# Who makes the low parts of the split weight blocks under the HGRN levels: VectorE or GpSimd

## The reference, cut to what matters

```python
def hgrn2_chunk_scan(q, k, logf, v):      # S_t = diag(f_t) S_{t-1} + k_t v_t^T, o_t = S_t^T q_t
...
    b = jnp.cumsum(fb, axis=2)
    decay = jnp.exp(jnp.where(incl, b_t - b_s, -jnp.inf))
    scores = jnp.einsum('nhtk,nhsk,nhtsk->nhts', qb, kb, decay)
    intra = jnp.einsum('nhts,nhsv->nhtv', scores, vb)
...
def hybrid_mixer(xn, w_in, ...):
    proj = jnp.einsum('bld,dc->blc', xn, w_in)
    q, zf_fwd, zf_bwd, inp, og, hy, gates = jnp.split(proj, IN_SPLITS, axis=-1)
```

## Time and profile before

| | |
|---|---|
| Times of the runs | 2528.5, 2533.27, 2532.15 us (median 2532.15) |
| Span of the profiled execution | 2527.7 us, first to last instruction |
| Busy share of TensorE, VectorE, ScalarE, GpSimd | 94%, 66%, 53%, 30% |
| Low parts by VectorE, line 343 | 398, of them 12 under the HGRN levels |
| Low parts by GpSimd, line 349 | 276 |

### The profile page before, as it was taken

One profiled execution on the slowest core, in us unless ns is written; L12 is line 12 of the kernel. 1 busy time (PEld: TensorE's weight loads), 2 busy tenths in 40 slices (PEclk: granted clock), 3 DMA queues, 4 the chain that ended last, 5 costly groups with the idle time before them and its releaser, 6 DMA issues.

```text
span 2527.7 us, 39068 instructions
## 1 busy us (share of the span) xinstructions
PE 2372.7 (94%) x15354; PEld 2141.8 (85%) x15354; DVE 1658.8 (66%) x3195; ACT 1342.3 (53%) x2494; POOL 770.8 (30%) x404
## 2 busy tenths in 40 slices
PE   6878998999999999998888888999999999999998
PEld 5876888999999888887867876789999999888886
DVE  4564457967777566665657475666977788566665
ACT  3344444468888444444533454244458888444443
POOL 3000002877776000000700053101887777000000
PEclk8888899999999999999999998999999999999999
DMA  5322334555555566664332343245555555566663
GB/s 175 122 94 70 94 99 153 176 177 165 165 163 170 179 192 193 190 191 140 117 122 87 125 135 109 67 150 159 184 176 162 165 162 163 184 192 192 191 193 123
DMA packets 108286, 383.36 MB, mean 152 GB/s; under 512 B 12975, under 2 KB 15840, under 8 KB 107528
## 3 DMA queue, kind: packets, MB, share of 16 engines
q1 hardware_dynamic: 108104, 380.86, 48.4%
HBM read 379.74 MB, written 1.06 MB: 151 GB/s over the span
## 4 chain that ended last, share of the span: by engine, by line
PE 81%; DVE 11%; ACT 4%; DMA 2%; issue 2%; POOL 0%; SPq 0%; DVEq 0%; ACTq 0%; POOLq 0%
PE psum L370 23%; PE psum L372 22%; PE psum L371 22%; PE psum L2042 2%; PE psum L402 2%; DVE weight_parts L343 2%; ACT weight_parts L338 1%; PE psum L616 1%; PE psum L2707 1%; PE psum L2487 1%; PE psum L1468 1%; PE psum L1029 1%; PE psum L1369 0%; PE psum L1199 0%; PE psum L1791 0%
## 5 line engine op out<-in xcount | busy, mean ns | idle before, releaser
L349 POOL TENSOR_TENSOR weight_parts<-weight_ring,weight_parts 128x1024 fp32r<-128x1024 f32 x276 | 670.5, 2440 | 505.7 <-ACT weight_parts L338 505.3
L370 PE MATMUL psum<-acts_high,weight_parts 128*128 128x256 f32 x2744 | 793.8, 289 | 22.4 <-DVE weight_parts L343 10.5
L372 PE MATMUL psum<-acts_high,weight_parts 128*128 128x256 f32 x2744 | 782.2, 285 | 0.0
L371 PE MATMUL psum<-acts_low,weight_parts 128*128 128x256 f32 x2744 | 781.8, 285 | 0.0
L338 ACT ACTIVATE weight_parts<-weight_ring 128x1024 fp32r<-128x1024 f32 x674 | 709.8, 1054 | 128.4 <-PE psum L372 60.7
L343 DVE TENSOR_TENSOR weight_parts<-weight_ring,weight_parts 128x1024 fp32r<-128x1024 f32 x398 | 487.6, 1226 | 306.6 <-ACT weight_parts L338 306.5
L370 PEld LDWEIGHTS psum<-acts_high,weight_parts 128*128 128x128 f32 x2744 | 531.6, 194 | 33.7 <-issue 12.5
L371 PEld LDWEIGHTS psum<-acts_low,weight_parts 128*128 128x128 f32 x2744 | 532.1, 194 | 1.3 <-issue 0.5
L372 PEld LDWEIGHTS psum<-acts_high,weight_parts 128*128 128x128 f32 x2744 | 532.0, 194 | 0.0
L370 PE MATMUL psum<-weight_parts,peer_coef 128*128 128x512 f32 x1024 | 404.0, 394 | 4.0 <-issue 3.9
L371 PE MATMUL psum<-weight_parts,peer_coef 128*128 128x512 f32 x1024 | 401.7, 392 | 0.0
(11 more groups left out here) (426 smaller groups left out, 3137.5 us busy)
## 6 DMA issues: line engine op xcount, KB each, us to landing
weight_ring<-in_peer_down SPq DMA_DIRECT2D x128, 512.0 KB, 3.6
weight_ring<-in_peer_up SPq DMA_DIRECT2D x128, 512.0 KB, 4.2
weight_ring<-in_peer_u SPq DMA_DIRECT2D x128, 512.0 KB, 3.6
weight_ring<-in_peer_v SPq DMA_DIRECT2D x128, 512.0 KB, 3.6
weight_ring<-in_w_in SPq DMA_DIRECT2D x88, 512.0 KB, 3.6
weight_ring<-in_w_out SPq DMA_DIRECT2D x16, 512.0 KB, 3.6
weight_ring<-in_peer_w_q SPq DMA_DIRECT2D x16, 512.0 KB, 4.1
weight_ring<-in_w_in_v SPq DMA_DIRECT2D x10, 512.0 KB, 3.5
```

The costliest lines, as they stand in the source:

```text
L349: q.e.tensor_tensor(self.low, self.ring, self.high.bitcast(F32), ALU.subtract).then_inc(*self.unit.ready.once())
L370: q.e.matmul(out, sh, mh, start=first, stop=False)
L371: q.e.matmul(out, sh, ml, start=False, stop=False)
L372: return q.e.matmul(out, sl, mh, start=False, stop=last)
```

## The change

`low_by` is set to "pool" before the units of `more()` are planned, and no longer only in `finish()`. So the 12 low parts under the levels go from VectorE's list to GpSimd's, at the same places between the rounds. Which blocks are whole, the loads, the roundings and the products stay as they were. `finish()` returns the mark of the last product, not that of the last product of a whole block.

```diff
+            c.low_by = "pool"
+
             def in_turns(units):
 
                 for n, _ in enumerate(units):
...
                 for _ in filler:
                     pass
                 c.whole = False
-                c.low_by = "pool"
                 c.flush(w[32], w[40])
-                return xn.whole_free
+                return c.last_product
```

## The result

| | before | after |
|---|---|---|
| median | 2531.63 us (6 runs, 2528.5 to 2534.11) | 2538.54 us (6 runs, 2536.17 to 2539.53) |
| span of the profiled execution | 2527.7 us | 2534.7 us |
| ratio, with its 95% interval | | 1.0033 [1.002, 1.0045] |

The forecast was +7.1 us, range 2530 to 2544; slower by over 0.2% had a chance of 0.58.

A forecast was written before the change was run, and what follows sets the result against it. The prediction took the chain of waits through VectorE's list to the second scores as the bound. Three pairs (1.1, 1.8, 1.65), the end (0.9) and TensorE's clock (1.65) gave +7.1 us, about 2539.2 us, range 2530 to 2544.

The forecast's parts named there:

- The bound: In the levels no engine is full; a chain of waits through load, rounding and VectorE's list to the second scores bounds.
- What is removed: 12 VectorE low parts of 1.14 us; second masked copy ends at T+4.9, not T+8.6 (T: end of a whole product).
- What is added: 12 GpSimd operations of 2.4 us, each costing VectorE 2.2 us of standing still where it meets parts or multiplications.
- The steps of pairs 2, 3 and 4 and the end: Second scores later by 1.1, 1.8 and 1.65 us in the three pairs; late low parts at the end add 0.9 us.
- TensorE's clock: Longer idle gap ahead of second scores makes the one quick pair slow (1.2 GHz): 1.40 plus 0.25, so +1.65 us.
- The total: +7.1 us on 2532.15, about 2539.2 us; +5.45 us without the clock's term.
- A: Rival: GpSimd's low parts cause no standing still that matters on VectorE; -4.4 us, 2527.7; chance 0.12.
- B: Rival: VectorE keeps its turn inside a run, GpSimd waits for the run's end; -1.4 us, 2530.8; chance 0.14.

The follow-up runs named there:

- Experiment 1: Kernel before with only the 4 low parts between the masked copies moved to GpSimd: ratio 0.9990 [0.998, 1.0001], stage 134.73 us for 138.88.
- experiment 5: Changed kernel, but each pair's third low part on GpSimd also waits for VectorE's last multiplication: ratio 1.0002 [0.999, 1.0013] to the kernel before.
- experiment 3: Kernel before with only the 3 low parts behind the multiplications (units 20, 26, 32) moved to GpSimd: ratio 1.0009 [0.9993, 1.0025].
- experiment 12: Repeat of experiment 3's kernel (only the 3 low parts behind the multiplications on GpSimd, against the kernel before): ratio 1.0002 [0.9989, 1.0014].
- experiment 2: Kernel before with only the 2 low parts behind the 8 parts (units 24, 30) moved to GpSimd: ratio 1.0008 [0.9993, 1.0023].
- experiments 6 to 8: Unread matmuls in TensorE's gaps, added to the changed kernel, the kernel before, and experiment 1's kernel: ratios to the kernel before 1.0038, 1.0014, 0.9986.
- experiments 9 to 11: Fewer unread matmuls, fitted to TensorE's gaps, in the changed kernel, the kernel before, and experiment 1's kernel: ratios to the kernel before 1.0034, 0.9996, 0.9985.

## Why the prediction was right

- **The bound.** The loop of load, rounding, copies, parts, exponentials, multiplications and scores sets the stage, and GpSimd's free time was no measure of the change's worth. Experiments 1 and 5 move the second scores by the amounts walked from it.
- **What is removed.** The second masked copy ended 3.7 us earlier in offsets from T, as said: 1346.49 against T = 1341.6 in the changed kernel. Experiment 1 keeps that gain and gives 1.0 to 1.6 us a pair.
- **What is added.** Standing still of 2.2 us: seven operations of the changed kernel took 3.28 to 3.42 us for 1.22, so 2.1 to 2.2. One place went otherwise, the eighth part of pair 4: there GpSimd lost one boundary (3.78 us) and then had the ports while VectorE waited 0.46 us for the exponential, so the first multiplication stood still for 1.6 us instead (3.91). The sum came out the same.

```profile
1393.21 3.78 POOL L349 TENSOR_TENSOR weight_parts<-weight_ring,weight_parts 128x1024 fp32r<-128x1024 f32 x1 [7.49 <-ACT weight_parts L338]
```

```profile
1395.23 3.91 DVE L2434 TENSOR_TENSOR hg_zf<-hg_q,hg_zf 128x2048 f32<-128x2048 f32 x1 [0.46 <-ACT hg_zf L2465]
```

- **The steps of pairs 2, 3 and 4 and the end.** +1.1, +1.7, +1.7 and +1.0 for 1.1, 1.8, 1.65 and 0.9. Their sum is 5.5 us, as forecast (5.45), and it is the part of the forecast that was right by its mechanism.
- **TensorE's clock.** This term was mis-sized, +4.2 us in the profiled stage for 1.65. Pair 3's second scores were slow before already, and I had taken one of the other two to change level. Both did: second scores of 3.52 and 3.75 us for 2.02 in pairs 2 and 4, and a whole product of 4.19 instead of 3.62 in pair 4. By pair that is +1.5, +0.4 and +2.3 us. The reason that I gave, the longer gap, is not shown. Pair 2's scores were slow behind a gap of 3.2 us here, but also behind 0.72 us in experiments 3 and 5, while experiment 12, the same kernel as 3, had them fast behind 0.75. Experiment 5 had all three slow with gaps no longer than before. The granted clock of 1366 to 1374 us was 0.50, where the earlier trace rows had 0.79:

```profile
1366.00:1374.00 8.00, 4.54 (x22) 0.50 0.00 0
```

- **The total.** That it met the forecast, 6.9 for 7.1, is partly luck: the interval of the ratio alone reaches from 5 to 11 us, and the clock's 1.65 is in the forecast without a run that shows it in the medians. The stage's 9.6 us is one execution. Either less of it is there on average, or the same slow spells hit the kernel before as well.
- **Rivals.** A is refuted by the stretched operations. B is refuted for the changed kernel, where GpSimd got the next boundary at 4 requests of 5; but its mechanism exists, and experiments 2, 3 and 12 show it. The argument with which I put B at 0.14, two operations of one line, was thin. Why the changed kernel met no wait as long as experiment 2's is argued, not shown: its parts end before the exponential is there, so VectorE's list has a gap at that place where GpSimd has not taken the boundary before it (0.46 us in pair 4).

## What to carry to other kernels

An operation moved to an idle GpSimd is not off VectorE's path while VectorE runs operations with two inputs in SBUF: price it as standing still for GpSimd's whole duration (2.2 us) where it took VectorE 1.1, and look for the places where it lands in a wait or under copies out of PSUM instead. Move work by its place in the list and not by its kind: moving 4 of these 12 low parts took 4 us off the stage, and 3 others cost the changed kernel 7.8 us by experiment 5, about what the whole change lost. Moved alone, the same 3 cost nothing that the runs could tell, because GpSimd lost its turn, so a place has to be tried in the kernel in which it will stand. Where a product waits for the GpSimd operation, look for a gap in VectorE's list ahead of it; without one it may not get its turn for a whole run of operations (15 us). That a gap cures this was not tried.

## What the runs showed of the hardware

- The two engines exclude each other for operations with two SBUF inputs (VectorE's took 3.28 to 3.42 us for 1.22 beside GpSimd's of 2.35), and who gets the next boundary is not fixed. In the changed kernel and its variants GpSimd mostly got it; in experiment 3's kernel it lost both boundaries in each of six pairs of two executions, and once it lost nine in a row, 12.9 us. The cause of the difference stays open.
- VectorE's masked copy (mask in SBUF, second source PSUM) does not take part: GpSimd's low part began in the middle of one, the two ran side by side for 1.1 us, the low part took 2.37 us and the copy 1.32 for 1.30. The page "SBUF — State Buffer" of the Trainium skill, "Who interferes with whom", says that a VectorE instruction with at most one SBUF input, outside certain fast modes, doesn't contend with GpSimd. The trace agrees; the prediction had found no row for it. The changed kernel's timelines:

```profile
1430.46 1.32 DVE L2456 COPY_PREDICATED hg_scores<-ident,psum 128x1024 f32<-128x1024 uint32 x1 [5.37 <-PE psum L2487]
```

```profile
1430.66 2.37 POOL L349 TENSOR_TENSOR weight_parts<-weight_ring,weight_parts 128x1024 fp32r<-128x1024 f32 x1 [7.73 <-ACT weight_parts L338]
```

- Behind idle times of this stage TensorE's granted clock was at 0.5 (1.2 GHz) in some places and at 1.0 in others, and the length of the idle time alone didn't tell which: 0.72 us ahead of scores of 3.75 us and 0.75 ahead of scores of 2.02 in two executions of one kernel, 2.45 us ahead of both in the kernel before. Where it fell it cost up to 2.3 us a pair. With matmuls that nobody reads all nine second scores of experiments 6 to 8 took 1.95 us, at the price of later scores; with the fitted counts of experiments 9 to 11, eight of nine took 1.95 or 2.02, at no price that the control's time shows.
